# Gate projections of a hybrid decoder layer as seven half-size products

## What is computed

```python
h = rmsnorm(x, norm_g); proj = h @ w_in            # queries, keys, values, z_a, z_b, r_a, r_b
y_a = (attn_a * silu(z_a)) @ w_pa                  # attn_a: dilated windows, 256 wide
y_b = (attn_b * silu(z_b)) @ w_pb                  # attn_b: block-sparse, 512 wide
merged = sigmoid(r_a + b_merge[:D]) * y_a + sigmoid(r_b + b_merge[D:]) * y_b
out = rmsnorm(x + merged @ w_out, final_g)
```

## Time and profile before

| | us |
|---|---|
| median of 3 runs (lowest, highest) | 444.41 (443.44, 444.61) |
| the profiled execution's own time | 443.48 |
| its span, first to last instruction | 441.7 |
| mean granted TensorE clock | 0.998 of 2.4 GHz |
| PE, DVE, ACT, POOL busy in the span | 431.6, 212.8, 198.5, 176.3 |

### The profile page before, as it was taken

The page is one execution under the profiler, slowest core; times in us unless marked ns, Lnnn a source line. Parts: engine busy times, 40 slices in busy tenths (PEclk is TensorE's granted clock), DMA queues, the critical chain, the costliest instruction groups (busy, mean ns, idle before and its releaser), DMA issues.

```text
span 441.7 us, 6258 instructions
## 1 busy us (share of the span) xinstructions
PE 431.6 (98%) x2377; PEld 374.5 (85%) x2377; DVE 212.8 (48%) x367; ACT 198.5 (45%) x401; POOL 176.3 (40%) x113
## 2 busy tenths in 40 slices
PE   7899999999999999999999999999999999999995
PEld 6789998899889988988888888888888888888885
DVE  3831244344435446757857664827025173083334
ACT  5743555335544464567555554533223543332111
POOL 4744442243243333646499543534355354200000
PEclk9999999999999999999999999999999999999999
DMA  8962234622452263024122022222222284210421
GB/s 284 286 192 96 96 96 83 159 96 95 91 150 97 96 168 110 25 96 143 49 95 96 0 73 96 96 72 96 95 71 96 95 261 156 113 66 0 149 90 47
DMA packets 40044, 48.31 MB, mean 109 GB/s; under 512 B 3768, under 2 KB 35536, under 8 KB 40016
## 3 DMA queue, kind: packets, MB, share of 16 engines
q1 hardware_dynamic: 37568, 47.72, 34.4%
q10 hardware_dynamic: 2448, 0.21, 0.4%
HBM read 39.48 MB, written 2.15 MB: 94 GB/s over the span
## 4 chain that ended last, share of the span: by engine, by line
PE 96%; DMA 2%; DVE 1%; ACT 1%; SPq 0%; issue 0%; DVEq 0%; ACTq 0%
PE ps L766 20%; PE ps L770 20%; PE ps L767 20%; PE ps L816 4%; PE ps L818 4%; PE ps L817 4%; PE ps L890 3%; PE ps L974 3%; PE ps L975 3%; PE ps L973 3%; PE ps L873 3%; PE ps L917 3%; PE ps L907 2%; DMA xs<-in_x 2%; PE ps L865 1%; PE ps L850 0%
## 5 line engine op out<-in xcount | busy, mean ns | idle before, releaser
L662 POOL TENSOR_TENSOR w_lo<-raw,w_hi 128x1024 fp32r<-128x1024 f32 (+1 forms) x59 | 138.1, 2342 | 175.4 <-ACT w_hi L990 175.4
L766 PE MATMUL ps<-hT_hi,w_hi 128*128 128x512 f32 x336 | 135.0, 402 | 1.1 <-DVE hT_lo L1241 1.1
L770 PE MATMUL ps<-hT_lo,w_hi 128*128 128x512 f32 x336 | 131.2, 390 | 0.0
L767 PE MATMUL ps<-hT_hi,w_lo 128*128 128x512 f32 x336 | 131.1, 390 | 0.0
L770 PEld LDWEIGHTS ps<-hT_lo,w_hi 128*128 128x128 f32 x336 | 63.1, 188 | 13.5
L766 PEld LDWEIGHTS ps<-hT_hi,w_hi 128*128 128x128 f32 x336 | 63.2, 188 | 11.2 <-issue 1.3
L767 PEld LDWEIGHTS ps<-hT_hi,w_lo 128*128 128x128 f32 x336 | 63.3, 188 | 9.9
L990 ACT CAST w_hi<-raw 128x1024 fp32r<-128x1024 f32 (+1 forms) x58 | 59.2, 1020 | 8.3 <-PE ps L770 5.4
L816 PE MATMUL ps<-w_hi,hT_hi 128*128 128x256 f32 x160 | 45.6, 285 | 0.0
L818 PE MATMUL ps<-w_lo,hT_hi 128*128 128x256 f32 x160 | 44.7, 279 | 0.0
L817 PE MATMUL ps<-w_hi,hT_lo 128*128 128x256 f32 x160 | 44.6, 279 | 0.0
(11 more groups left out here) (148 smaller groups left out, 665.6 us busy)
## 6 DMA issues: line engine op xcount, KB each, us to landing
raw<-in_w_in SPq DMA_DIRECT2D x25, 1024.0 KB, 4.9
KTs<-KTs SPq DMA_DIRECT2D x20, 256.0 KB, 3.4
raw<-in_w_out SPq DMA_DIRECT2D x4, 1024.0 KB, 4.8
xs<-in_x SPq DMA_DIRECT2D x4, 512.0 KB, 5.3
raw<-in_w_pb SPq DMA_DIRECT2D x4, 512.0 KB, 4.1
res<-in_x SPq DMA_DIRECT2D x4, 512.0 KB, 3.9
out<-weighted SPq DMA_DIRECT2D x8, 256.0 KB, 2.1
raw<-in_w_in SPq DMA_DIRECT2D x2, 512.0 KB, 8.9
```

The lines of the kernel that those rows point to most:

```text
L662: nc.gpsimd.tensor_tensor(ring(w_lo, n, kt), src, ring(w_hi, n, kt).bitcast(F32), ALU.subtract).then_inc(lo_ready, 1)
L766: pe.matmul(out, wh, hh, start=(k == 0), stop=False)
L767: pe.matmul(out, wl, hh, start=False, stop=False)
L770: return pe.matmul(out, wh, hl, start=False, stop=(k == kts - 1))
```

## The change

Chunk 0 of r_a and r_b stays as it was. Chunks 1 to 3 of each, six in all, are computed by the Winograd form of Strassen's scheme: h^T and the weights are cut into 2 x 2 quarters (4 row tiles x 256 positions, 4 row tiles x 128 columns), and seven products of quarters or of sums of quarters replace eight. A product is 4 row tiles x 3 matmuls of 256 columns. After the last step (NS is now 40) all three remaining kinds of work form one list of operations, `OPS`, numbered by o: 4 half branch products for each 256 columns (`y`), 7 products for each of the six chunks (`r`), in the order y0 r0 r1 y1 r2 r3 r4 r5 y2 y3.

- The four sums of h quarters ("folds", 1024 elements per partition each) are formed once: folds 0, 1 and 3 on DVE at slots 35, 36 and 39 with three, two and two additions, fold 2 on POOL (`fold_third`, four parts from slot 37 on; its last part subtracts the low part). ACT copies their high parts (`fold_high`), DVE subtracts the low parts of 0, 1 and 3 (`fold_low`).
- The four sums of weight quarters of a chunk, 512 elements each, are formed on DVE (`sum_quarters`) seven and six operations ahead of the chunk.
- Products go to four PSUM banks in turn, 256 columns each. ACT copies product 0 out, and DVE forms the outputs with eight additions (`combine`); ACT then applies the tanh (`squash`).
- The high parts of an operation's weights are copied by ACT six operations ahead, into a ring of eight slots; all low parts, those of w_out included, are POOL's (`split_low`), in the order of the loads.
- ysum is one buffer instead of two, and the low part of a merged tile comes two operations later.

The diff, cut:

```diff
+SEVEN = [(b, c) for c in range(1, ND // 2) for b in range(2)]
+NSEV = len(SEVEN)
+PARTS = [("y", 0), ("r", 0), ("r", 1), ("y", 1), ("r", 2), ("r", 3), ("r", 4), ("r", 5), ("y", 2), ("y", 3)]
+OPS = []
+for kind, c in PARTS:
+    if kind == "r":
+        OPS += [("r", c, p) for p in range(7)]
+    else:
+        OPS += [("y", 2 * c + j, half) for j in range(2) for half in range(2)]
+OP_OF = {op: o for o, op in enumerate(OPS)}
+R_DONE = OP_OF[("r", NSEV - 1, 6)] + 1
+NSLOT = 8
+AHEAD = 6
...
+        PRODUCT_BANKS = [0, 1, PVB, MB]
+        FOLDED = {1: 1, 2: 2, 3: 0, 6: 3}
+        SUM_AT = {3: 1, 1: 2, 2: 3, 5: 4}
...
+        def slot_free_wait(eng, o):
+            if o < NSLOT:
+                eng.wait_ge(projected, NS - 3 + o // 2)
+            else:
+                eng.wait_ge(consumed, o - NSLOT + 1)
...
+            def fold_third(part):
+                hi, lo = (folded[:, 2, e, :, :] for e in range(2))
+                full = folded_sum(2)
+                hi11, lo11 = (h_quarter(t, 0, 0).bitcast(F32) for t in (hT_hi, hT_lo))
+                hi21, lo21 = (h_quarter(t, 1, 0).bitcast(F32) for t in (hT_hi, hT_lo))
+                if part == 0:
+                    pool.wait_ge(valued, NH)
+                    nc.gpsimd.tensor_tensor(full, hi11, hi21, ALU.subtract).then_inc(folded_full[2], 1)
+                elif part == 1:
+                    pool.wait_ge(folded_full[2], 1)
+                    nc.gpsimd.tensor_tensor(full, full, lo11, ALU.add).then_inc(folded_full[2], 1)
+                elif part == 2:
+                    pool.wait_ge(folded_full[2], 2)
+                    nc.gpsimd.tensor_tensor(full, full, lo21, ALU.subtract).then_inc(folded_full[2], 1)
+                else:
+                    pool.wait_ge(folded_hi[2], 1)
+                    nc.gpsimd.tensor_tensor(lo, full, hi.bitcast(F32), ALU.subtract).then_inc(folded_lo[2], 1)
...
             for n in range(1, NS):
...
                 if n - 2 == SCALED[HEX]:
                     add_residue_groups()
+                if n - 2 >= FOLD_SLOT:
+                    fold_third(n - 2 - FOLD_SLOT)
+            for part in range(NS - 2 - FOLD_SLOT, 4):
+                fold_third(part)
+            for item in SPLITS:
+                split_low(item)
...
+            def product(o):
+                _, q, p = OPS[o]
+                out = product_out(q, p)
+                split_wait(OPS[o])
+                g = 7 * q + p
+                if g == 0:
+                    proj_taken_wait(pe, NS - 2)
+                elif g == 1:
+                    proj_taken_wait(pe, NS - 1)
+                elif g == 2:
+                    pe.wait_ge(values_taken, NH)
+                elif g == 3:
+                    pe.wait_ge(misc_taken, len(MISC))
+                    pe.wait_ge(turn_taken[2], third_begun[0])
+                else:
+                    pe.wait_ge(taken[(g - 4) % 7], (g - 4) // 7 + 1)
+                if p in FOLDED:
+                    n = FOLDED[p]
+                    if q == 0:
+                        pe.wait_ge(folded_hi[n], 1)
+                        pe.wait_ge(folded_lo[n], 1)
+                    hh, hl = (folded[:, n, e, :, :] for e in range(2))
+                else:
+                    hh, hl = (h_quarter(t, *{0: (0, 0), 4: (0, 1), 5: (1, 1)}[p]) for t in (hT_hi, hT_lo))
+                wh, wl = slot_of(w_hi, o), slot_of(w_lo, o)
+                for k in range(4):
+                    pe.matmul(out, wh[:, k, :], hh[:, k, :], start=(k == 0), stop=False)
+                    pe.matmul(out, wh[:, k, :], hl[:, k, :], start=False, stop=False)
+                    last = pe.matmul(out, wl[:, k, :], hh[:, k, :], start=False, stop=(k == 3))
+                last.then_inc(consumed, 1)
...
+            def split_high(item):
...
+                if item[0] == "wo":
+                    k = item[1]
+                    if k < 2:
+                        act.wait_ge(gated_lo, 6)
+                        act.wait_ge(valued, NH)
+                    else:
+                        act.wait_ge(consumed, R_DONE)
+                    nc.scalar.copy(wo("hi", k), raw_out(k)).then_inc(hi_ready, 1)
+                    return
+                if item[0] == "r" and item[2] in SUM_AT:
+                    act.wait_ge(sum_ready, 4 * item[1] + SUM_AT[item[2]])
+                o = OP_OF[item]
+                slot_free_wait(act, o)
+                nc.scalar.copy(slot_of(w_hi, o), op_source(item)).then_inc(hi_ready, 1)
+            def fold_high(n):
+                act.wait_ge(folded_full[n], 3 if n in (0, 2) else 2)
+                nc.scalar.copy(folded[:, n, 0, :, :], folded_sum(n)).then_inc(folded_hi[n], 1)
...
+                for n in {FOLD_SLOT + 2: (0,), FOLD_SLOT + 3: (1,), FOLD_SLOT + 4: (2,)}.get(s, ()):
+                    fold_high(n)
                 if s >= NS - 2:
+                    for item in SPLITS[:4] if s == NS - 2 else SPLITS[4:AHEAD]:
+                        split_high(item)
                 for n in gated_in(s - 2):
...
+            for o in range(len(OPS) + 3):
+                if o == 0:
+                    fold_high(3)
+                for item in SPLITS:
+                    if DUE[item] == o:
+                        split_high(item)
+                if o and o - 1 < len(OPS) and OPS[o - 1][0] == "r":
+                    take_product(o - 1)
+                if o > 1 and o - 2 < len(OPS) and OPS[o - 2][0] == "r" and OPS[o - 2][2] == 6:
+                    squash(OPS[o - 2][1], 1)
+                if o > 2 and OPS[o - 3][0] == "y" and OPS[o - 3][2] == 1:
+                    merged_high(OPS[o - 3][1])
...
+            def sum_quarters(q, part):
+                one, two, last = sums[:, 0, :, :], sums[:, 1, :, :], sum_last[:, :, :]
+                if part == 0:
+                    s, count = raw_waits(("r", q))
+                    dve.wait_ge(s, count)
+                    if q:
+                        dve.wait_ge(lo_ready, split_count(("r", q - 1, 3)))
+                    else:
+                        dve.wait_ge(folded_lo[0], 1)
+                    nc.vector.tensor_tensor(one, quarter(q, 0, 1), quarter(q, 0, 0), ALU.subtract).then_inc(sum_ready, 1)
+                    dve.wait_ge(sum_ready, 4 * q + 1)
+                    nc.vector.tensor_tensor(two, quarter(q, 1, 1), one, ALU.subtract).then_inc(sum_ready, 1)
+                else:
+                    if q:
+                        dve.wait_ge(lo_ready, split_count(("r", q - 1, 5)))
+                    third = quarter(q, 0, 1)
+                    nc.vector.tensor_tensor(third, quarter(q, 1, 1), third, ALU.subtract).then_inc(sum_ready, 1)
+                    dve.wait_ge(sum_ready, 4 * q + 2)
+                    nc.vector.tensor_tensor(last, quarter(q, 1, 0), two, ALU.subtract).then_inc(sum_ready, 1)
...
+            def fold(n):
+                hi = [h_quarter(hT_hi, i, j).bitcast(F32) for i in range(2) for j in range(2)]
+                lo = [h_quarter(hT_lo, i, j).bitcast(F32) for i in range(2) for j in range(2)]
+                full = [folded_sum(m) for m in range(4)]
+                add = nc.vector.tensor_tensor
+                if n == 0:
+                    dve.wait_ge(scored, _s)
+                    add(full[0], hi[2], hi[3], ALU.add).then_inc(folded_full[0], 1)
+                    dve.wait_ge(folded_full[0], 1)
+                    add(full[0], full[0], lo[2], ALU.add).then_inc(folded_full[0], 1)
+                    dve.wait_ge(folded_full[0], 2)
+                    add(full[0], full[0], lo[3], ALU.add).then_inc(folded_full[0], 1)
...
+            def combine(o):
...
+                src = product_out(q, p)
+                if p:
+                    dve.wait_ge(consumed, o + 1)
+                if p == 1:
+                    dve.wait_ge(first_copied, q + 1)
+                    if q:
+                        dve.wait_ge(c12_ready, q)
+                    add(u_two[:, :], first_copy[:, :], src, ALU.add).then_inc(u_two_ready, 1)
+                elif p == 2:
+                    dve.wait_ge(u_two_ready, q + 1)
+                    add(u_three[:, :], u_two[:, :], src, ALU.add).then_inc(u_three_ready, 1)
+                elif p == 3:
+                    if q == 0:
+                        dve.wait_ge(gated_lo, 6)
+                        dve.wait_ge(valued, NH)
+                    dve.wait_ge(u_three_ready, q + 1)
+                    add(right[:, 256:512], u_three[:, :], src, ALU.add).then_inc(c22_ready, 1)
+                    add(right[:, 0:256], u_two[:, :], src, ALU.add).then_inc(u_four_ready, 1)
+                elif p == 4:
+                    add(left[:, 0:256], first_copy[:, :], src, ALU.add).then_inc(c11_ready, 1)
+                elif p == 5:
+                    add(left[:, 256:512], u_three[:, :], src, ALU.add).then_inc(c21_ready, 1)
+                elif p == 6:
+                    dve.wait_ge(u_four_ready, q + 1)
+                    add(right[:, 0:256], right[:, 0:256], src, ALU.add).then_inc(c12_ready, 1)
...
```

(60 more changed lines are left out.)

303 lines of the change are left out of this document (185 added, 118 removed).

## The result

The changed kernel takes 462.68 us (median of 4 runs, 462.49 to 463.01) against 444.05 us for the kernel before, beside it on the same chip. The ratio is 1.042, with a 95% interval from 1.040 to 1.044. The forecast was 459.0 in a range from 441 to 468, slower with a chance of 0.80. The profiled execution took 462.69 us with a span of 460.9; before they were 443.48 and 441.7. The comparison to explain is therefore 19.2 us of span.

A forecast was written before the change was run, and what follows sets the result against it. PE, busy 98% of the span, was taken to bound the kernel. Sum: 443.48 - 5.6 + 5.8 + 2.8 + 2.5 + 5.5 + 3 + 1.5 = 459.0 us, range 441 to 468.

The forecast's parts named there:

- the rule of turns: DVE additions with both inputs in SBUF and POOL instructions wait for each other and alternate when both queue.
- The hole before step 37: Fold(0) ahead of DVE's z operation delays the PSUM bank; PE starts step 37 at 283.9, not 278.1: +5.8 us.
- The gain of the products: Six gate chunks on PE, 84 matmuls of 256 columns instead of 48 of 512 each: 5.6 us saved (4.8 to 6.3).
- First branch product: PE, ready at 300.2, waits until 302.9 for weights queued behind POOL's fourth fold part: +2.8 us (0 to 5).
- Products 2 and 4 of chunk 0: PE waits for POOL's split at product 2 (+1.7) and again at product 4 (+0.8): +2.5 us (0 to 5).
- Product 5 of chunk 0: PE waits for DVE's addition that takes product 1 out of its PSUM bank: +5.5 us (0 to 8).
- The last chunks: Output weights use up POOL's lead before chunk 4; product 5 waits again in the last chunk: +3 us (0 to 6.5).
- Clock: Matmuls behind two long PE holes run at the lower clock for a while: +1.5 us (0 to 3.5).
- A: Rival: only the first hole, before step 37; later waits fall within the lead of seven products; 444 to 447, chance 0.16.
- B: Rival: chained DVE fold operations keep the port, POOL doesn't get in between, hole of 1.3; 439.2 us, chance 0.14.
- C: Rival: POOL-bound throughout, at 11.7 us a chunk or 1.59 per product; 466 and more, chance 0.08 together with D.
- D: Rival: 256-column pace of products over 0.1295, no gain at all; 459 + 5.6, chance 0.08 together with C.

The follow-up runs named there:

- POOL's share small: Against the changed kernel, POOL's first two operations of fold 2 handle 8 elements instead of 1024, so fold 2 isn't computed in full; 460.41 us.
- POOL's order changed: Against the changed kernel, fold(0) in slot 34, POOL's last fold part behind four branch splits, first two output weight tiles split ahead of chunk 2; 458.72 us.

## Why the prediction came out

- **What bounds it, and the rule of turns**: right. The first addition of fold(0) was forecast to end at 276.4, the second at 279.7, the third at 283.1 and z at 283.8; they ended at 277.0, 280.4, 283.6 and 284.2, 0.4 to 0.7 late, with PE 0.6 late already at 273 us. The hole before step 37 measured 5.6 for 5.8.
- **The gain of the products**: 4.8 for 5.6. The term lay at the lower end of its bounds, because the starts are 0.120 us apart, as in the last output groups of the earlier trace rows, not 0.1185. The 7.1 us that the prediction sets beside it stand on a formula that the Trainium skill, "TensorE: Matmul & The Clock Gate", section "Back-to-back issue gap", gives for a single matmul by itself, not for a stream of weight loads and matmuls like this one.
- **First branch product**: 1.5 for 2.8; the chain behind POOL's last fold part was right (POOL idle 10.6 us for ACT's copy), but the weights were ready at 304.2 instead of 302.9, and PE itself was free at 302.7 instead of 300.2, 2.0 us of that by the slow matmuls that the clock term stands for.
- **Products 2 and 4 of chunk 0**: nothing for 2.5. I had DVE finish fold(3) at 312.1; it did at 310.0, and by the rows the turns it waited for were POOL's shorter branch splits, which cost it less. The low part of product 2 was ready at 314.7 instead of 315.7, and PE came to it at 315.4 instead of 314.0, late by what had held it up before.
- **Product 5 of chunk 0**: 5.5 for 5.5. The experiments with the sums later (hole 1.7) and without folds (no hole) show both causes that the prediction named, the sums ahead of the addition and the fold work ahead of the sums.
- **The last chunks**: 4.8 for 3, between the bounds, and in chunk 3 as well as in chunk 4. The output weights as the cause: shown, by the kernel that moved them behind the chunks. In chunk 3 DVE's last sum waits for an output-weight subtraction, in chunk 4 its first sum waits for a low part that POOL does behind them:

```profile
362.75 5.66 POOL L837 TENSOR_TENSOR wo_first<-raw,wo_first 128x1024 fp32r<-128x1024 f32 x2
...
363.26 2.90 DVE L1677 TENSOR_TENSOR sum_last<-raw,sums 128x512 f32<-128x512 f32 x1
373.51 1.70 DVE L1668 TENSOR_TENSOR sums<-raw 128x512 f32<-128x512 f32 x1 [3.31 <-POOL w_lo L842]
```

- **Clock**: the mis-sized term, 5.8 for 1.5. Three holes, not two, had slow matmuls behind them, and each took 1.6 to 2.0 us. The stretch behind the first:

```profile
284.30:288.40 4.10, 4.01 (x10) 3.21 (x11) 4.10 (x2) 1.05 (x2) 4.10 (x2) 0.50 0.32 97
288.40:293.80 5.40, 5.40 (x25) 4.49 (x24) 5.37 (x7) 2.96 (x5) 0.26 (x1) 0.99 0.36 125
```

The granted clock is 0.50, the lower level of 1.2 GHz, for ten matmuls of 0.43 us each between starts, then 2.4 GHz again. Even a hole of 3.6 us (chunk 4) was followed by matmuls at half pace; holes of 1.4 us and less had a single longer first matmul. The Trainium skill, "TensorE: Matmul & The Clock Gate", section "HAM oscillation — how this bites in real kernels", says that longer PE-idle gaps bring the clock down and the next work starts cold; the trace agrees, with these numbers. But the length of a hole does not give the price by itself (lengths as in the table of PE): behind 2.6 us (POOL's share small) and 2.3 us (fold(0) early with output weights early) came 1.6 and 1.5 us of slow matmuls, behind the 5.6 us of the kernel with the output weights late 2.9 us, and behind the 3.7 us of the kernel without folds and the 3.6 us in chunk 2 of the kernel with POOL's order changed the granted clock stayed at 1.00.

The sum of forecast terms was 15.5, of measured ones 19.2. Errors of both signs stand in it: gain and clock too favourable by 5.1, holes too unfavourable by 4.0 in the start (12.6 for 16.6) and too favourable by 1.8 at the end, and 0.8 that no term stood for. That the forecast of 459.0 came within 4 us of the measured time is thus in part luck; the sign and the largest terms, the two holes of 5.6 and 5.5, are not.

Of the rivals, A (only the first hole) fell on the trace, which has a second hole of 5.5 us, and on the move of fold(0): the time that a hole gives is not spare, since DVE works through it. B fell on DVE's rows: POOL did get in after each chained operation. C, POOL as the bound throughout, did not come out: POOL is busy 34.7 of 40.3, 15.5 of 15.5 and 29.5 of 31.0 us behind 325 us, but PE has no gap in the first and third of these stretches and loses 4.8 us in holes over all of them. What holds of it is that POOL has little to spare there: its first output weights made a hole of 2.2 to 4.4 us at both places that they had among the chunks. D is excluded by the pace.

What stays open: why DVE was let in between POOL's output-weight subtractions in the changed kernel and not in two of its variants; why some holes of 3.6 and 3.7 us left the clock as it was; and how the 15.8 us of the folds divide between DVE and POOL on one side and ACT's copies on the other. None of the kernels tried beats the one before; the best complete one took 458.7 us.

## What to carry to other kernels

When PE is bound by columns, an arithmetic saving of one in eight is worth what the smaller instructions leave of it (here 4.8 of 65 us), and the additions that buy it must have room on engines that don't share a port: count VectorE's operations with two SBUF inputs and GpSimd's as one queue, in time order, and look for what PE needs behind them. Moving such an operation within the busy stretch moves the wait (fold(0) later: nothing); taking it out of the stretch shortens the path, by less than it took there (fold(0) earlier: 3.3 of 8.7 us). Price a PE hole as the hole plus slow matmuls behind it: here mostly 1.3 to 2.9 us behind holes of 2.3 us and more, and in some cases nothing.

## What the runs showed of the hardware

- DVE can be shut out for long: an addition of 512 elements that takes 0.69 us alone took 15.19 and 11.85 us while POOL ran subtractions end to end. A wait of POOL for its own previous instruction brought it back to 1.42 us.
- POOL isn't slowed by a DVE operation that is kept waiting: four subtractions of 1024 elements took 9.49 us (2.37 each) while DVE's addition waited, and 10.47 us (2.62 each) in the changed kernel, where DVE got in.
- PE's clock falls behind holes and comes back at a price of 1.6 to 2.0 us a time in the changed kernel and 1.3 to 2.9 us in its variants, in matmuls of 256 columns as of 512; behind two holes of 3.6 and 3.7 us it stayed at 1.00. A filler in the first hole took the slow matmuls away.
